# Token-major projections in blocks of 512 columns, and attention row sums by transposes and a VectorE reduction

## The reference

```python
# even layer: gated chunk mixer (A) beside a bidirectional S5 recurrence (B)
u, v, g_a, xs, g_b = split(h @ w_in)          # h = modulated rms_norm, 1280 x 1024
y_a = chunk_gmlp(u, layer_norm(v)) * silu(g_a)
y_b = s5_bidir(xs);  y_b = y_b * sigmoid(y_b @ w_glu + b_glu) * silu(g_b)
x, ctx = x + gt * (mix @ w_out), ctx + gtc * (mix @ w_out)
# odd layer: attention, 8 query heads of 128, 2 key heads
q, k, v, gate = split(h @ w_in)
q, k = rope(rms_norm(q)), rope(rms_norm(k))   # context keys without rope
p = softmax(q @ k.T / sqrt(128))              # 1024 queries x 1280 keys
x = x + gt * ((p @ v) * silu(gate)) @ w_out
return rms_norm(x, final_g)
```

## Time and profile before

| | |
|---|---|
| time before, median of 3 runs | 1287.96 us (1287.51 to 1289.15) |
| the profiled execution | 1286.58 us, its span 1284.8 us |
| mean granted TensorE clock | 0.988 |
| PE busy | 1218.3 us, 95% of the span, 8450 matmuls |
| DVE, ACT, POOL busy | 831.6, 513.4, 470.1 us |
| DMA | 130.08 MB |

### The profile page before, as it was taken

One profiled execution on the slowest core, in us unless ns is written; L12 is line 12 of the kernel. 1 busy time (PEld: TensorE's weight loads), 2 busy tenths in 40 slices (PEclk: granted clock), 3 DMA queues, 4 the chain that ended last, 5 costly groups with the idle time before them and its releaser, 6 DMA issues.

```text
span 1284.8 us, 20932 instructions
## 1 busy us (share of the span) xinstructions
PE 1218.3 (95%) x8450; PEld 1074.9 (84%) x8450; DVE 831.6 (65%) x1420; ACT 513.4 (40%) x960; POOL 470.1 (37%) x383
## 2 busy tenths in 40 slices
PE   2999999999999889999999999999999999999997
PEld 2888788888889749999999988877788888888997
DVE  5798839899725172146466899359777777776125
ACT  3535446110025141134433432157566666665012
POOL 4600000000000004331112112159999999998332
PEclk9899999999999899999999999999999999999999
DMA  9835766326413942113111212320000000000402
GB/s 338 323 107 165 205 194 225 119 103 229 149 49 134 338 155 66 34 67 132 34 34 34 66 43 82 115 90 9 9 17 9 17 17 9 17 9 9 165 33 100
DMA packets 89231, 130.08 MB, mean 101 GB/s; under 512 B 12944, under 2 KB 59408, under 8 KB 88336
## 3 DMA queue, kind: packets, MB, share of 16 engines
q1 hardware_dynamic: 79312, 113.96, 26.4%
q10 hardware_dynamic: 9824, 14.80, 3.4%
HBM read 97.81 MB, written 30.93 MB: 100 GB/s over the span
## 4 chain that ended last, share of the span: by engine, by line
PE 77%; DMA 8%; DVE 6%; ACT 3%; POOL 3%; SPq 2%; issue 1%; ACTq 0%; POOLq 0%; DVEq 0%
PE ps L1770 10%; PE ps L1772 10%; PE ps L1771 10%; PE ps L1781 5%; PE ps L1782 5%; PE ps L1783 5%; PE ps L2029 3%; PE ps L2063 3%; PE ps L2064 2%; PE ps L2065 2%; PE ps L2051 2%; PE ps L2049 2%; PE ps L2052 2%; PE ps L2050 2%; PE ps L2094 2%; PE ps L2095 2%
## 5 line engine op out<-in xcount | busy, mean ns | idle before, releaser
L1770 PE MATMUL ps<-w_hi,a_hi 128*128 128x256 f32 x896 | 257.4, 287 | 6.6 <-DVE b_lo L1140 3.0
L1771 PE MATMUL ps<-w_lo,a_hi 128*128 128x256 f32 x896 | 255.5, 285 | 0.0
L646 POOL TENSOR_TENSOR region_b<-region_b,region_d 128x256 f32<-128x256 f32 x40 | 29.7, 749 | 496.6 <-DVE region_d L1446 496.6
L1772 PE MATMUL ps<-w_hi,c_lo 128*128 128x256 f32 x736 | 209.2, 284 | 0.0
L1770 PEld LDWEIGHTS ps<-w_hi,a_hi 128*128 128x128 f32 x896 | 174.1, 194 | 9.0 <-issue 5.0
L1771 PEld LDWEIGHTS ps<-w_lo,a_hi 128*128 128x128 f32 x896 | 174.1, 194 | 0.0
L639 POOL TENSOR_TENSOR w_lo<-weight_ring,w_hi 128x2048 fp32r<-128x2048 f32 x16 | 74.1, 4628 | 199.3 <-ACT w_hi L694 199.3
L1772 PEld LDWEIGHTS ps<-w_hi,c_lo 128*128 128x128 f32 x736 | 142.3, 193 | 0.0
L1542 DVE TENSOR_REDUCE small<-ps 128x1 f32<-128x1280 f32 x64 | 95.3, 1488 | 69.9 <-PE ps L2029 69.9
L1781 PE MATMUL ps<-a_hi,w_hi 128*128 128x512 f32 (+1 forms) x384 | 138.5, 361 | 1.2 <-ACT region_d L694 1.2
L1782 PE MATMUL ps<-b_lo,w_hi 128*128 128x512 f32 (+1 forms) x384 | 136.7, 356 | 0.0
(11 more groups left out here) (234 smaller groups left out, 2917.7 us busy)
## 6 DMA issues: line engine op xcount, KB each, us to landing
weight_ring<-in_w_mod SPq DMA_DIRECT2D x10, 2048.0 KB, 9.2
weight_ring<-in_we_in SPq DMA_DIRECT2D x10, 1024.0 KB, 5.9
weight_ring<-in_wo_in SPq DMA_DIRECT2D x10, 1024.0 KB, 5.3
weight_ring<-cop_t_scratch SPq DMA_DIRECT2D x4, 1536.0 KB, 7.4
region_c<-in_w_mod SPq DMA_DIRECT2D x2, 2048.0 KB, 18.8
bop_scratch<-region_d ACTq DMA_DIRECT2D x16, 256.0 KB, 3.6
cop_t_scratch<-region_d SPq DMA_DIRECT2D x8, 512.0 KB, 7.4
weight_ring<-bop_scratch SPq DMA_DIRECT2D x2, 2048.0 KB, 10.4
```

The source lines that it names most:

```text
L1770: te.matmul(o, th, wh[:, k], start=first and k == 0, stop=False)
L1771: te.matmul(o, th, wl[:, k], start=False, stop=False)
L1772: last = te.matmul(o, tl, wh[:, k], start=False, stop=stop and k == KT - 1)
```

## The change

The five token-major projections move 512 columns per matmul. A unit of weights is now one half of k (512 rows) x 512 columns, again 1 MB, so that a PSUM tile needs two units, first the low half of k and then the upper. Tiles go in groups that fit the four PSUM banks: the low half for the group, then the upper half for it. Evacuations and additions become 512 columns wide. Everything that was tied to quarters of a projection (releases of slots, weight rounding, norms of x1, `to_features`, `k_transposes`, head norms) gets a new place. In attention, the four one-column matmuls become four 128x128 transposes, and DVE adds them up over 128 columns before the reciprocal. The core of the diff:

```diff
-        otmp = RD[:, 0:512].rearrange("p (a n) -> p a n", a=2)
+        otmp = RD[:, 0:1024].rearrange("p (a n) -> p a n", a=2)
...
+                elif kind in wide:
...
+                    src = wt[0][512 * (b % 2):512 * (b % 2) + 512,
+                                a + 512 * (b // 2):a + 512 * (b // 2) + 512].rearrange("(k p) n -> p k n", p=P)
...
             off_ring_load(2, s_ld_v)
+            off_ring_load(3, s_ld_ws)
             ring_load("v", 1)
-            off_ring_load(3, s_ld_ws)
...
-                if t == 4 and q < 3:
-                    weights_rest((("out0", 2), ("out0", 3), ("kv", 0))[q])
+                if q == 0 and t in (5, 9):
+                    weights_rest(("out0", 2 if t == 5 else 3))
+                if q == 1 and t == 0:
+                    weights_rest(("kv", 0))
...
                     if t == 8:
                         h1_evac(1)
+                    if t == 9:
+                        weights_round(("kv", 1))
...
-                if q == 3 and t == 2:
+                if q == 1 and t == 2:
                     dve.wait_ge(s_rt, 3)
                     row_rstd(slice(0, 2))
                     x1_norm(0)
                     x1_norm(1)
-                if q == 3 and t == 3:
+                if q == 1 and t == 4:
                     for k in range(KT):
                         h1_full(0, k)
-                if q == 3 and t == 5:
-                    h1_rest(0)
-                if q == 3 and t == 6:
+                if q == 1 and t == 5:
                     dve.wait_ge(s_rt, 4)
                     x1_rstd(slice(2, 6))
                     x1_norm(2)
                     x1_norm(4)
-                if q == 3 and t == 7:
+                    h1_rest(0)
                     for k in range(KT):
                         h1_full(1, k)
...
-            def token_part(weights, bank, c0, tokens, ks=range(KT), first=True, stop=True):
+            def wide_part(weights, bank, tokens, ks):
...
-                o = ps[:, bank, c0:c0 + QC]
+                o = ps[:, bank, :]
                 for k in ks:
                     th, tl = tokens(k)
-                    te.matmul(o, th, wh[:, k], start=first and k == 0, stop=False)
+                    te.matmul(o, th, wh[:, k % 4], start=k == 0, stop=False)
...
+                    mods(3)
+                if k == 1:
+                    mod_cols(3)
             ws.append(split_of(("v", 1)))
...
+            w_low, w_up = split_of(("kv", 0)), None
+            for group in ((0, 1, 2, 3), (4,), (5,), (6, 7, 8, 9)):
+                for t in group:
...
+                    last = wide_part(w_low, 4 + t % 4, lambda k: h1_of(k, t), range(4))
...
+                if w_up is None:
                     to_features(2, *x1n)
+                    w_up = split_of(("kv", 1))
+                for t in group:
+                    wide_part(w_up, 4 + t % 4, lambda k: h1_of(k, t), range(4, KT)).then_inc(s_kv_mm, 1)
...
                 for h in range(HPK):
-                    last = te.matmul(ps[:, 7, h:h + 1], psum_p[:, i % 2, P * h:P * h + P], onec, start=True, stop=True)
+                    last = tr(ps[:, 7, P * h:P * h + P], psum_p[:, i % 2, P * h:P * h + P])
...
+                for half in range(2 if j == 2 * LT - 1 else 1):
...
+                    n_ = QC if j == 2 * LT - 1 else 512
...
+                    g.tensor_tensor(xs_, xs_, zt[:, j % 4, QC * half:QC * half + n_], ALU.add).then_inc(s_z_ok, 1)
```

More of the change, by code:

```diff
@@ L318, in build @@
         done_when |= {("bop", b): (s_b_mm, 16 * (b + 1)) for b in range(2)}
-        done_when |= {("kv", b): (s_kv_mm, TT * (b + 1)) for b in range(2)}
+        wide = ("v", "out0", "kv", "q", "out1")
+        blocks = [("out0", 0), ("out0", 1), ("kv", 0), ("q", 0), ("q", 1), ("out1", 0)]
+        done_when |= {(kind, 2 * b): (s_w_half, i + 1) for i, (kind, b) in enumerate(blocks)}
+        done_when[("kv", 1)] = (s_kv_mm, TT)
+        for b in range(2):
+            done_when |= {("out0", 2 * b + 1): (s_o_mm, TT * (b + 1)), ("q", 2 * b + 1): (s_q_mm, LT * (b + 1))}
+        done_when[("out1", 1)] = (s_z_mm, LT)
         for b in range(4):
-            done_when |= {("ct", b): (s_c_mm, 4 * (b + 1)), ("out0", b): (s_o_mm, (TT, 2 * TT, 4 * TT, 4 * TT)[b]), ("q", b): (s_q_mm, LT * (b + 1)),
-                          ("gate", b): (s_g_mm, 4 * (b + 1)), ("out1", b): (s_z_mm, (LT, 2 * LT, 4 * LT, 4 * LT)[b])}
+            done_when |= {("ct", b): (s_c_mm, 4 * (b + 1)), ("gate", b): (s_g_mm, 4 * (b + 1))}
         source = {"v": (we_in, W), "xs": (we_in, 3 * W), "u": (we_in, 0), "ga": (we_in, 2 * W), "gb": (we_in, 4 * W),
@@ L1953, in _ @@
                 for t in range(4):
-                    last = token_part(ws, 4 + t, 0, lambda k: mix_of(k, t), ks)
+                    last = wide_part(w_up, 4 + t, lambda k: mix_of(k, t), ks)
                     if ks[-1] == KT - 1:
                         last.then_inc(s_o_mm, 1)
-            for j, (q, t) in list(enumerate(out_order))[4:]:
-                if q not in wo:
-                    wo[q] = split_of(("out0", q))
-                ws = wo[q]
-                pe.wait_ge(s_o_t, j - 3)
-                token_part(ws, 4 + j % 4, 0, lambda k: mix_of(k, t)).then_inc(s_o_mm, 1)
-                if q == 3 and t in (3, 7):
-                    to_features(t // 4, *x1n)
@@ L1967, in _ @@
-            pe.wait_ge(s_o_t, 4 * TT)
-            for j in range(2 * TT):
-                part, t = divmod(j, TT)
-                if t == 0:
-                    ws = split_of(("kv", part))
-                if j in (0, 2, 6):
-                    pe.wait_ge(s_h1_lo, {0: 8, 2: 16, 6: 24}[j])
-                if j >= 4:
-                    pe.wait_ge(s_kv_ev, j - 3)
-                    if j - 4 < TT:
-                        pe.wait_ge(s_hd_sq, 2 * (j - 3))
-                token_major_split(ws, 4 + j % 4, lambda k: [z(k, t * P, P)[:, 0] for z in (h1_high, h1_low)], s_kv_mm)
-                if j == 2:
+            for b in range(2):
+                groups = ((4,), (5,), (6, 7, 8, 9))
+                if b:
+                    w_low, w_up = split_of(("out0", 2)), None
+                    groups = ((0, 1, 2, 3),) + groups
+                for group in groups:
+                    for t in group:
+                        j = TT * b + t
+                        pe.wait_ge(s_o_t, j - 3)
+                        last = wide_part(w_low, 4 + j % 4, lambda k: mix_of(k, t), range(FB))
+                        if t == TT - 1:
+                            last.then_inc(s_w_half, 1)
+                    if w_up is None:
+                        w_up = split_of(("out0", 3))
+                    if b and group[-1] == TT - 1:
+                        to_features(1, *x1n)
+                    for t in group:
+                        j = TT * b + t
+                        wide_part(w_up, 4 + j % 4, lambda k: mix_of(k, t), range(FB, KT)).then_inc(s_o_mm, 1)
+                    if b and group == (4,):
+                        to_features(0, *x1n)
@@ L1980, in _, with k_transposes @@
                     to_features(2, *x1n)
-            def k_transposes():
+                    w_up = split_of(("kv", 1))
+                for t in group:
+                    wide_part(w_up, 4 + t % 4, lambda k: h1_of(k, t), range(4, KT)).then_inc(s_kv_mm, 1)
+            def k_transposes(js):
                 pe.wait_ge(s_k_ok, LT)
-                pe.wait_ge(s_kv_ev, 2 * TT)
-                for j in range(6):
+                pe.wait_ge(s_kv_ev, TT)
+                for j in js:
                     h, q = divmod(j, 3)
```

275 lines of the change are left out of this document (155 added, 120 removed).

## The result

The changed kernel takes 1266.03 us (median of 4 runs, 1261.84 to 1272.89) against 1287.74 for the kernel before, measured beside it. The ratio is 0.9847, with a 95% interval of 0.9826 to 0.9869, so about 20 us less, and the forecast was 1265. Its profiled execution took 1264.96 us with a span of 1263.2, against 1284.8. In the sum the forecast was right. By stages it was not, and the errors cancelled.

A forecast was written before the change was run, and what follows sets the result against it. PE was taken to bound the kernel, with POOL nearly a second bound in attention. Terms 1.6 + 6.2 + 1.9 + 5.1 + 2.5 + 4.6 gave 21.9 us off 1286.6; adjusted to the median, 1266.1, stated as 1265, range 1256 to 1273.

The forecast's parts named there:

- The price of a matmul: Token-major projections: one 512-column matmul saves 13.3 ns against two of 256, 23.0 us for 1728 pairs.
- Rival (D): Projections: width gives nothing on its own, only 2.5 ns kept per pair, so about 1282 us; chance 0.04.
- v: v projection: 1.6 us gained from 120 pairs behind the modulation row's wait; earlier gains only lengthen that wait.
- Before out0: Recurrence, from the end of v up to out0: forecast gain 0.
- out0 and glu: 6.2 us gained: 6.4 from matmuls and 1.3 of a glu wait, against 1.5 for `to_features(0)`.
- kv: kv projection: 1.9 us gained, 4.0 from matmuls and a wait, minus 2.1 waiting for norms delayed by POOL's low part.
- rival (C): kv and attention: two late chains, PE idles and its clock falls; 1274 us, about 1270 with one; chance 0.20.
- my sign for being right in kv: kv: PE idle about 2 us ahead of the transposes, released by DVE's norms, with POOL's `w_lo` over DVE's small instructions.
- q: q projection: 5.1 us from matmuls; the 0.75 wait at `k_transposes` goes, the 0.99 end wait grows by as much.
- Attention: Row sums by transposes: 2.5 us gained, 6.9 minus 3.0 for waits and 1.4 lost waiting for POOL.
- exactly free: Attention: DVE's added 0.72 us per group just fits between the reciprocal's end and PE's need, in eight groups.
- out1: out1 and tail: 4.6 us gained, 5.1 from matmuls and 0.5 from row sums, minus 1.0 for the last evacuation.

The follow-up runs named there:

- split_256: The changed kernel with each 512-column matmul of the token-major projections issued as two of 256 columns: 1288.6 us, ratio 1.0004 to the kernel before.
- row_sums_old: The changed kernel with the row sums of before, four one-column matmuls and a reciprocal from PSUM: 1266.98 us, ratio 0.9834 to the kernel before.
- narrow_rows: The changed kernel with the first unit of out0 loaded in rows of 1 KB by two DMAs: 1266.49 us, ratio 0.9837 to the kernel before.
- kv_low_dve: The changed kernel with the low part of ("kv", 1) on DVE, after `h1_rest(1)`, instead of POOL: 1257.06 us, ratio 0.9778 to the kernel before.

## Why the prediction held, point by point

**The price of a matmul** was right: 13.3 ns for each pair, 23.0 us. The starts 0.2267 apart and the 22.6 us of `split_256` show it. Rival (D), that width gives next to nothing, is out. (Its price slips: 23.0 − 4.3 is 18.7 and not 18.0, so 5.1 and not 5.5. Nothing hangs on it.)

**v** was wrong by 2.3 us. I costed the idle stretch ahead of the modulation row at its present 2.55 us. It came to 2.76, and this time the clock fell behind it:

```profile
76.00:80.00 4.00, 3.87 (x11) 3.10 (x12) 3.83 (x7) 0.65 (x3) 0.00 (x0) 0.57 0.42 152
```

The next 24 matmuls took 7.23 us instead of 5.44, which ate the 1.6. `row_sums_old` has the same 2.76 and no low clock from 74 to 82. But six of the seven profiles with the changed kernel's order in v have the low clock there, and neither of the two with the old order has it, behind idle stretches of 2.55 and 2.27 us. So this term goes with the change in most executions, and I had no term for it.

**Before out0** I forecast nothing and 3.7 us appeared. PE idles 2.44 us where it idled 3.85, since the unit could be rounded 9.1 us after the issue of its load instead of 10.8. That gives 1.4. The 12 records of matmuls behind it and the step to out0 took 2.49 us instead of 4.16, at a clock of 1.00 instead of 0.50. That gives 1.7, and the other 0.6 lies ahead of the idle stretch. Of eleven profiles of this study with the rounding in this place, three with rows of 1 KB have 3.35 to 3.85, and eight with rows of 2 KB have 2.09 to 3.81. The wide row may help, but this wasn't settled. Nor is the gain chance alone: from the end of v to out0, nine profiles of changed kernels that round here take 319.1 to 323.3 us (320.2 in this one), the two with the old projections 323.9 and 324.3, and `narrow_rows` has the 319.1. Where it comes from stays open.

**out0 and glu** gave 8.8 instead of 6.2. Its first 48 matmuls of before ran partly at half clock, and took 8.0 us (434.07 to 442.07) instead of 5.8. The changed kernel had 1.00 there. Without these 2.2 us it is 6.6. Of eight profiles of changed kernels with 512 columns and the rounding at its place, four have 154.5 us for out0 and glu, as this one has, and four have 156.2 to 156.9. The wait for `to_features(0)`, for which I took 1.5, was 0.57.

**kv** is the step that failed: "POOL takes the low part of that unit from E+5.9 to E+10.5. Meanwhile DVE should compute the inverse roots from E+7.4". With E at 584.7, POOL began at E+4.95, one microsecond earlier than I had reckoned. And I had not written down when `h1_rest(1)` ends. Its second instruction meets POOL's addition to x1 (585.52 to 587.20) and takes 1.79 us instead of 0.68. In `kv_low_dve`, where this happens too and no pass follows, the eighth starts at 595.47, E+5.97, so a pass begun at E+5.9 as I had it would still have stood ahead of it. The pass did not meet the inverse roots but the last parts of `h1_rest(1)`, for which PE waits without cover. I had named this case as rival (C), with its low clock, at −0.6 less 2.6 for kv, which is 7.2 under the undisturbed 4.0. It measured 7.2 under `kv_low_dve`, where I had taken 2.1. So the forecast's mechanism in kv was wrong and that half of (C) was right. The price of the meeting was about right (4.6 us for an instruction that meets the pass, 5.01 measured), only its place was not. The idle stretch of 2 us ahead of the transposes, my sign for being right in kv, didn't come.

**q** behaved as forecast: the waits at `k_transposes` went, and the last one grew by 0.73. **Attention** gave 2.2 instead of 2.5. The reduction took 678 ns, near the upper bound of 688 and not at the 600 that I took, but with less handover than I took: from its start to the end of the reciprocal it is 0.89 us, of which the reciprocal had 0.17 before, so the chain grew by the 0.72 that I had reckoned. What failed is "exactly free". It left nothing for the 0.05 us between reciprocal and transposes, and DVE's `p_lo` ahead of the reduction took 0.86 us instead of 0.79 in the groups shown. So a group of the steady part lost 0.10 to a wait that shows only in the weight loads, and 0.06 to longer transposes. My sign for (C) in attention, that these transposes stand on DVE's reciprocal in most groups, came true, at a tenth of its price. **out1** gave 4.9 instead of 4.6.

That the sum came out at 21.6 for 21.9 is luck. The stages that fell short lost 7.0 us against the forecast (v 2.3, kv and q 4.4, attention 0.3), and those that gave more gave 6.6 (before out0 3.7, out0 and glu 2.6, out1 0.3). Of the 6.6, the 3.7 and the 2.2 of the clock in out0 had no term in the forecast. A part is also luck of the one execution: the stretch before out0 took 321.2 us on average in the nine profiles named, 1.0 more than here, and out0 and glu took about 2 more in half of the eight. The ratio of the runs gives 19.7 us, with an interval of 17 to 22.

## What to carry to other kernels

Where PE sets the end, take the price of a matmul from starts, at both widths, and multiply: it held to a few per cent for 1728 pairs. Where one engine's long pass can block another's short instructions, write down for each such pass what the other engine does in that window, with start and end, and move it or give it away when a microsecond's error in the timetable would put it on the path; here that was worth 7 us. After a change that shortens one chain, look again at every place where an inferred slack was "exactly enough".

## What was unexpected of the hardware

A granted clock of about 0.5 followed idle stretches of PE of 2.8 us (76) and 4.5 us (595.75), but not always: after 2.44 us at 428 the changed kernel kept 1.00, and `kv_low_dve` fell to 0.65 (433 to 441) after 2.09 us at the same place, and `row_sums_old` kept 1.00 after 2.76 us at 76. So one profile can't price such a stretch, and kernels that differ by 2 us need several. A wait for the operand of a transpose can be nearly invisible in the waits of PE (in the changed kernel, for the transposes of the inverse sums, 1.6 us in three instances) and stand with the weight loads instead (6.4 us in 13).
